# Where in a row the moved activations start: 256 columns at 32 bytes past a multiple of 64, 512 columns at a multiple of 64

## What is computed

```python
def first_block(x, mem, ...):
    mem_n = _rmsnorm(mem, mem_norm_w)
    for l in range(DEPTH):                                    # DEPTH = 1
        h = h + _hybrid_mixer(_rmsnorm(h, mix_norm_w[l]), ...)            # w_in, w_out
        h = h + _memory_cross_attn(_rmsnorm(h, xattn_norm_w[l]), mem_n, ...)   # wq, wk, wv, wo
        h = h + _conv_ffn(_rmsnorm(h, ffn_norm_w[l]), ffn_up[l], ffn_conv_w[l], ffn_down[l])
    return _rmsnorm(h, final_norm_w)

def swiglu(h, w_gu, w_down):
    gate, up = jnp.split(h @ w_gu, 2, axis=-1)
    return (jax.nn.silu(gate) * up) @ w_down

def ffn_half_step(x, mods, g, w_gu, w_down):
    shift, scale, gate = mods
    return x + 0.5 * gate * swiglu(modulated_norm(x, g, shift, scale), w_gu, w_down)

def second_block(x, c, ctx, c_ctx, ...):
    for l in range(DEPTH_2):                                  # DEPTH_2 = 2
        x = ffn_half_step(x, mx[0:3], ...); ctx = ffn_half_step(ctx, mc[0:3], ...)
        # l = 0: Fourier and gating mixer of x and of ctx; l = 1: attention of x over x and ctx
        x = x + mx[5] * out_x
        x = ffn_half_step(x, mx[6:9], ...)
        if not last:
            ctx = ctx + mc[5] * out_c
            ctx = ffn_half_step(ctx, mc[6:9], ...)
    return rms_norm(x, g_final)
```

## Time and profile before

| | before |
|---|---|
| median of three runs (lowest, highest) | 2164.09 us (2163.41, 2167.21) |
| the profiled execution: its own time, its span | 2168.27 us, 2166.5 us |
| TensorE busy in the span | 2098.2 us (97%), 13881 records |
| VectorE, ScalarE, GpSimd busy | 985.2, 817.4, 224.9 us |
| mean granted TensorE clock | 0.991 |
| read from HBM | 310.87 MB, mean 144 GB/s |

### The profile page before, as it was taken

One profiled execution on the slowest core, in us unless ns is written; L12 is line 12 of the kernel. 1 busy time (PEld: TensorE's weight loads), 2 busy tenths in 40 slices (PEclk: granted clock), 3 DMA queues, 4 the chain that ended last, 5 costly groups with the idle time before them and its releaser, 6 DMA issues.

```text
span 2166.5 us, 31783 instructions
## 1 busy us (share of the span) xinstructions
PE 2098.2 (97%) x13881; PEld 1821.0 (84%) x13882; DVE 985.2 (45%) x1270; ACT 817.4 (38%) x1046; POOL 224.9 (10%) x185
## 2 busy tenths in 40 slices
PE   7988999999999999999999999999999999999998
PEld 6985998999978888788887888888788888869998
DVE  6768555767522322354542332253233235645444
ACT  5742454555522222244332222243212224345444
POOL 1000001413101011100101001111100110001011
PEclk9999999999999999999999999999999999999999
DMA  6425544454631333452343332243334222364543
GB/s 236 156 80 195 209 180 180 167 190 158 222 150 67 112 148 114 158 206 98 126 156 132 114 113 82 94 156 136 137 126 155 76 93 93 114 253 156 173 177 109
DMA packets 53708, 313.97 MB, mean 145 GB/s; under 512 B 5952, under 2 KB 12353, under 8 KB 23745
## 3 DMA queue, kind: packets, MB, share of 16 engines
q1 hardware_dynamic: 50848, 308.99, 39.7%
q10 hardware_dynamic: 2720, 2.95, 0.4%
HBM read 310.87 MB, written 1.05 MB: 144 GB/s over the span
## 4 chain that ended last, share of the span: by engine, by line
PE 87%; DVE 6%; ACT 3%; issue 2%; DMA 0%; SPq 0%; POOL 0%; DVEq 0%; ACTq 0%; POOLq 0%
PE psum L258 27%; PE psum L260 26%; PE psum L259 26%; PE psum L1646 3%; ACT w_hi L234 2%; DVE w_lo L242 1%; PE psum L1293 1%; PE psum L1283 1%; PE psum L1307 0%; DMA raw<-in_w_in_r 0%; PE psum L895 0%; DVE xn_lo L1811 0%; PE psum L896 0%; DVE work L431 0%; PE psum L1714 0%
## 5 line engine op out<-in xcount | busy, mean ns | idle before, releaser
L258 PE MATMUL psum<-xn_hi,w_hi 128*128 128x256 f32 (+1 forms) x2600 | 864.5, 332 | 18.2 <-DVE xn_lo L438 8.4
L259 PE MATMUL psum<-xn_lo,w_hi 128*128 128x256 f32 (+1 forms) x2600 | 853.1, 328 | 0.0
L260 PE MATMUL psum<-xn_hi,w_lo 128*128 128x256 f32 (+1 forms) x2600 | 852.7, 328 | 0.0
L242 DVE TENSOR_TENSOR w_lo<-raw,w_hi 128x2048 fp32r<-128x2048 f32 (+1 forms) x246 | 510.0, 2074 | 453.2 <-ACT w_hi L234 452.3
L258 PEld LDWEIGHTS psum<-xn_hi,w_hi 128*128 128x128 f32 x2600 | 496.6, 191 | 74.4 <-issue 23.1
L259 PEld LDWEIGHTS psum<-xn_lo,w_hi 128*128 128x128 f32 x2600 | 497.1, 191 | 43.1 <-issue 1.2
L260 PEld LDWEIGHTS psum<-xn_hi,w_lo 128*128 128x128 f32 x2600 | 496.9, 191 | 42.2
L234 ACT ACTIVATE w_hi<-raw 128x2048 fp32r<-128x2048 f32 (+1 forms) x246 | 421.7, 1714 | 212.8 <-PE psum L260 134.8
L258 PE MATMUL psum<-h_hi,w_hi 128*128 128x512 f32 (+1 forms) x913 | 312.5, 342 | 1.6 <-POOL h_lo L1621 1.6
L259 PE MATMUL psum<-h_lo,w_hi 128*128 128x512 f32 (+1 forms) x913 | 310.9, 341 | 0.0
L260 PE MATMUL psum<-h_hi,w_lo 128*128 128x512 f32 (+1 forms) x913 | 310.8, 340 | 0.0
(11 more groups left out here) (375 smaller groups left out, 1334.6 us busy)
## 6 DMA issues: line engine op xcount, KB each, us to landing
raw<-in_mod SPq DMA_DIRECT2D x72, 1024.0 KB, 4.9
raw<-in_a_up SPq DMA_DIRECT2D x42, 1024.0 KB, 4.9
raw<-in_b_up SPq DMA_DIRECT2D x42, 1024.0 KB, 4.9
raw<-in_ffn_up SPq DMA_DIRECT2D x22, 1024.0 KB, 4.9
raw<-in_a_down SPq DMA_DIRECT2D x32, 704.0 KB, 4.1
raw<-in_b_down SPq DMA_DIRECT2D x32, 704.0 KB, 4.1
raw<-in_ffn_down SPq DMA_DIRECT2D x16, 704.0 KB, 4.1
raw<-in_wo SPq DMA_DIRECT2D x8, 1024.0 KB, 5.0
```

Of the source, the lines that this page charges most:

```text
L242: dve.tensor_tensor(w_lo[:, slot, 0:size], raw[:, raw_slot(("main", g)), 0:size], w_hi[:, slot, 0:size].bitcast(F32), ALU.subtract).then_i ...
L258: pe.matmul(out, lh, rh, start=first, stop=False, skip_group_check=group)
L259: pe.matmul(out, lh, rl, start=False, stop=False, skip_group_check=group)
L260: return pe.matmul(out, ll, rh, start=False, stop=last, skip_group_check=group)
```

## The change

The rows of xn_hi and xn_lo become 528 columns long (2112 bytes, a multiple of 64). Where the normed activations are moved 256 columns at a time they are written and read 8 columns (32 bytes) further on: columns 8 to 263 for X, 264 to 519 for C. Where they are moved 512 at a time they stand 16 columns (64 bytes) further on, 16 to 527. The hidden values of the two narrow feed-forwards stand at columns 8 to 263 of h_hi and h_lo, whose rows stay 512 long; the wide ones stay at 0. q2 and the halves of wide jobs read 256 columns out of a wide row, at a multiple of 64. The memory's values for wv, which are stationary there, lie at the narrow place. To make room, mrow becomes columns 7680 to 7935 of the tensor work.

The rows of the program are the same on every engine, in the same order with the same waits; only in the Fourier and gating branch two writes each of ScalarE and VectorE over two k read 128x2x512 in place of 128x1024.

The diff, cut; what is left out puts one of the new slices in place of X, C, XC or `0:self.w` in the same way:

```diff
+NARROW_AT, WIDE_AT = 8, 16
...
-        xn_hi = sb("xn_hi", [P, KT, 2 * T], F32R)
-        xn_lo = sb("xn_lo", [P, KT, 2 * T], F32R)
+        xn_hi = sb("xn_hi", [P, KT, 2 * T + WIDE_AT], F32R)
+        xn_lo = sb("xn_lo", [P, KT, 2 * T + WIDE_AT], F32R)
...
-        mrow = sb("mrow", [P, 256])
+        mrow = work[:, 7680:7936]
...
+        NARROW_X = slice(NARROW_AT, NARROW_AT + T)
+        NARROW_C = slice(NARROW_AT + T, NARROW_AT + 2 * T)
+        WIDE_X = slice(WIDE_AT, WIDE_AT + T)
+        WIDE_XC = slice(WIDE_AT, WIDE_AT + 2 * T)
...
+                self.at = span.start + (WIDE_AT if wide else NARROW_AT)
...
-                        t, o = slice(h * T, (h + 1) * T), slice(self.span.start + h * T, self.span.start + (h + 1) * T)
+                        t, o = slice(h * T, (h + 1) * T), slice(self.at + h * T, self.at + (h + 1) * T)
...
+                self.xn_span = WIDE_XC if w > T else NARROW_X
+                self.h_span = XC if w > T else NARROW_X
...
-                        pe_feature_major(pe, up, xn_hi, xn_lo, slice(0, self.w))
+                        pe_feature_major(pe, up, xn_hi, xn_lo, self.xn_span)
...
-                    pe_feature_major(pe, down, h_hi, h_lo, slice(0, self.w), n_tiles=1, k_tiles=HALF, before_k=hidden_k,
+                    pe_feature_major(pe, down, h_hi, h_lo, self.h_span, n_tiles=1, k_tiles=HALF, before_k=hidden_k,
...
-                        out = h_hi[r, s.c:s.c + 1, 0:self.w]
+                        out = h_hi[r, s.c:s.c + 1, self.h_span]
...
-                t = slice(h * T, (h + 1) * T)
+                t, o = slice(h * T, (h + 1) * T), slice(WIDE_AT + h * T, WIDE_AT + (h + 1) * T)
...
-                act.activation(xn_hi[:, k, :], o_t[:, k, :], ACT.Copy).then_inc(o_hi, 1)
+                act.activation(xn_hi[:, k, WIDE_XC], o_t[:, k, :], ACT.Copy).then_inc(o_hi, 1)
...
-            pe_feature_major(pe, jobs["w_out"], xn_hi, xn_lo, X, before_k=mixed_k)
+            pe_feature_major(pe, jobs["w_out"], xn_hi, xn_lo, NARROW_X, before_k=mixed_k)
...
-            pe_token_major(pe, jobs["wv"], C)
+            pe_token_major(pe, jobs["wv"], NARROW_C)
...
-            pe_feature_major(pe, jobs["q2"], xn_hi, xn_lo, X, after_chunk=beside_queries)
+            pe_feature_major(pe, jobs["q2"], xn_hi, xn_lo, WIDE_X, after_chunk=beside_queries)
```

More of the change, by code:

```diff
@@ L322, in build, with __init__ @@
             made, scaled, split, squared, added = 0, 0, 0, 0, 0
-            def __init__(self, span, scale, shift=None, out=None, tiles=1, direct=None, pool_low=False, early_table=False, first_tile=None):
+            def __init__(self, span, scale, shift=None, out=None, tiles=1, direct=None, pool_low=False, early_table=False, first_tile=None,
+                         wide=False):
                 self.pool_low = pool_low
@@ L446, in pool_lows @@
                     pool.wait_ge(n_hi, self.split_base + k + 1)
-                    pool.tensor_tensor(xn_lo[:, k, self.span], nrm[:, k, 0:self.w], xn_hi[:, k, self.span].bitcast(F32),
+                    o = slice(self.at, self.at + self.w)
+                    pool.tensor_tensor(xn_lo[:, k, o], nrm[:, k, 0:self.w], xn_hi[:, k, o].bitcast(F32),
                                        ALU.subtract).then_inc(n_lo, 1)
@@ L1210, in post_act_high @@
             act.wait_ge(post_scaled, i + 1)
-            act.activation(xn_hi[:, pair(i), X], z[:, pair(i), :], ACT.Copy).then_inc(post_hi, 1)
+            act.activation(xn_hi[:, pair(i), NARROW_X], z[:, pair(i), :], ACT.Copy).then_inc(post_hi, 1)
         def post_pe_sums(pe, i):
@@ L1700, in __init__ @@
             def __init__(self, scale, shift, job, tiles=1):
-                super().__init__(XC, scale, shift, tiles=tiles)
+                super().__init__(XC, scale, shift, tiles=tiles, wide=True)
                 self.job, self.i = job, HalfNorm.count
@@ L1717, in pe_last @@
             def pe_last(self, pe, s, act_hi, act_lo, n_tiles, k_tiles, k_order):
+                first = WIDE_AT if act_hi is xn_hi else 0
                 for h in range(2):
-                    t = slice(h * T, (h + 1) * T)
+                    t = slice(first + h * T, first + (h + 1) * T)
                     for n in range(n_tiles):
@@ L1926, in pe_first @@
                 for h, t in ((1, C), (0, X)):
+                    o = slice(WIDE_AT + t.start, WIDE_AT + t.stop)
                     for k in k_order:
@@ L2326, in _ @@
             pe.wait_ge(at_lo, att1.heads)
-            pe_feature_major(pe, jobs["wo"], xn_hi, xn_lo, X, in_halves={3: pe_tile_by_tile})
+            pe_feature_major(pe, jobs["wo"], xn_hi, xn_lo, NARROW_X, in_halves={3: pe_tile_by_tile})
             ffn.pe(pe)
@@ L2337, in _ @@
             feed3.pe(pe, late=lambda: mod_turn(pe), closing=n24)
-            pe_feature_major(pe, jobs["k2"], xn_hi, xn_lo, XC, in_halves={0: n24.pe_first})
+            pe_feature_major(pe, jobs["k2"], xn_hi, xn_lo, WIDE_XC, in_halves={0: n24.pe_first})
             def turn_keys():
@@ L2383, in _ @@
             pe.wait_ge(at_lo, att1.heads + att2.heads)
-            pe_feature_major(pe, jobs["wo2"], xn_hi, xn_lo, X, in_halves={3: pe_tile_by_tile})
+            pe_feature_major(pe, jobs["wo2"], xn_hi, xn_lo, NARROW_X, in_halves={3: pe_tile_by_tile})
             n25.pe(pe)
```

55 lines of the change are left out of this document (27 added, 28 removed).

## The result

| | before | after |
|---|---|---|
| median (lowest, highest) | 2165.01 us (2163.41, 2167.61), 6 runs | 2176.09 us (2171.32, 2178.86), 6 runs |
| ratio of the runs | | 1.0045, 95% interval 1.0034 to 1.0055 |
| the profiled execution's time, its span | 2168.27, 2166.5 | 2172.27, 2170.5 |
| mean granted TensorE clock | 0.991 | 0.993 |

A forecast was written before the change was run, and what follows sets the result against it. TensorE's matmul pace was taken as the bound: 4848 x 3.0 ns = 14.5 us off, under 1 us back for first writes, 1 us at risk, giving 2149.6 us from 2164.1; forecast's own range 2132 to 2159, whole range 2110 to 2180.

The forecast's parts named there:

- What bounds the kernel: Whole program: TensorE busy for 97% of the span; the 256-column stages go at the pace of the matmul.
- The extra 13.3 ns: Each full-clock three-pass matmul: 120 ns against 106.7 for 256 columns, 227 against 213.3 for 512; laid to feeding the array.
- 4848 matmuls, from 120 to 117 ns: 256-column matmuls with xn or h moving from the new start: 3.0 ns less each, 14.5 us in all.
- two reads that come to rest against each other: Weight load and moved stream overlap and settle at 120 ns; moving one by 32 bytes (3.3 ns) could give 116.7.
- 227 ns for 512 columns and 120 ns in q2, both as before: Expected profile of the changed kernel: wide matmuls and q2 keep their paces.
- the longer rows: Rows of 528 split writes of two k into two pieces of 512 in the Fourier branch; only six subtractions there.
- the bound of one more piece of 64 bytes: High bound for a moved 256-column matmul: 17 pieces touched instead of 16, so 126.7 ns.
- 14.5 us of gain: Narrow stages: 4848 x 3.0 ns off; first feed-forward's up half from 64.7 to 63.1 us.
- one (109 ns): Rival: the whole feed overhead goes in the 4848 matmuls, pace 109.3 ns, 51.9 us less, 2112; chance 0.14.
- Two (no effect): Rival: the feed reads 256 columns equally fast from any start; 2164 within 5 us; chance 0.19.
- Three: Rival: one more 64-byte piece for each of the 4848 narrow matmuls, 6.67 ns each, 32.3 us slower, 2196; chance 0.19.
- mrow, writes, the stationary side: mrow's copy unchanged; first writes at the new place perhaps 1 us; 192 value-projection matmuls of the first attention priced at nothing.

The follow-up runs named there:

- ahead_32: The kernel before with 32 unused bytes ahead of the raw buffers, so weights and activations all move 32 bytes on together; 2165.1 us, ratio 0.9997.
- rows_528: The changed kernel with both offsets set to 0: xn rows 528 columns long, every moved start a multiple of 64 bytes; 2175.7 us, 1.0040 of before.
- behind_64: The kernel before with 64 unused bytes between the split weights and all tensors behind them, so activations start 64 bytes further on; 2165.0 us, ratio 1.0003.
- behind_32: The kernel before with 32 unused bytes between the split weights and all tensors behind them, so activations start 32 bytes further on; 2185.8 us, ratio 1.0091.
- weights_0: The kernel before with the split weights as one tensor 128 columns longer and mrow in work, weights at their old places; 2165.7 us, ratio 1.0002.
- weights_32: weights_0 with the narrow stages' split weights 32 bytes further on, activations and wide stages' weights unmoved; 2160.7 us, 0.9977 of before.

## Why the prediction was wrong, step by step

- **What bounds the kernel:** right. TensorE's pace decides, and both signs went into the time.
- **The extra 13.3 ns are a matter of feeding:** borne out so far as they change with addresses alone; what in the feed it is was not shown.
- **4848 matmuls, from 120 to 117 ns:** the size was right for the 1056 with h moving (116.7). For the 3792 with xn moving it was 118.2, so 1.8 ns where I had 3.0; together about 10 us by pace in place of 14.5. The reason was only half right. I took the start "32 bytes past a multiple of 64" for the cause; ahead_32 has it and stays at 120, rows_528 and behind_64 have it not and go at 117. My picture of two reads that come to rest against each other fits the distance between weights and activations, and the two beats of behind_64 too, but no run shows the reads.
- **The step that failed:** "227 ns for 512 columns and 120 ns in q2, both as before". The wide matmuls had no term at all; I asked only what a shift of 32 bytes does to the 4848, and priced the longer rows as two split writes. With 2112 bytes from k to k the distance to the weights, which lie 512 bytes apart, changes with k, and the wide matmuls lost 5.0 ns each: 3217 x 5.0 = 16 us. I kept the bound of one more piece of 64 bytes (6.7 ns) for the narrow ones only. The first chunk of q2 shows the same omission the other way: its start stayed at a multiple of 64, and it went at 5.49 / 47 = 117 ns (1847.10 to 1852.59 us), not 120.
- **14.5 us of gain:** mis-sized at the stage level. The paces give 12 us, the stages 8 to 10; some is lost where TensorE waits. The first up half of the first feed-forward, 64.7 us for which I had named 63.1, takes 64.3 in after (362.56 to 426.87 us). There every second chunk of before had 301 to 321 ns from its last start to the next chunk's first, and after has 368 to 387: the wait at the chunk's end takes part of what the matmuls save.
- **Rivals:** one (109 ns) did not come; no distance tried gave less than 116.7 as a mean, and the lowest beat that held was 113.4, in parts of behind_64. Two (no effect) came only as the sum of two effects, in behind_64. The 298 against 291 ns that I read for it are durations; the starts of the token-major matmuls were 119.9 ns apart in before. Three had the sign of the time right for the wrong matmuls: the loss is on the 512-column ones. Its price of 6.67 ns is nearly what they pay in behind_32 (226.8 to 233.3), but behind_64 pays 2.3, so the count of pieces is not shown.
- **mrow, writes, the stationary side:** nothing measurable for mrow, by weights_0. The writes take as long at the new place: 32 of ScalarE at a median of 417 ns before and after, 24 of VectorE at 418 and 420. The token-major matmuls went from 119.9 to 118.2 ns in after, among them the 192 of the first attention's value projection, which I priced at nothing, from 120.0 to 117.8.

## What to carry to other kernels

When a change touches a layout, list every reader of the tensor with its count, those whose own start seems unchanged too, and give each a term: here the 3240 matmuls that were left alone by the stated purpose decided the sign. Read the pace, first start to last start over a stretch without waits, for each width before and after; two opposite changes of 2 to 3% in it are invisible in busy times and can cancel in the total. And test an address hypothesis with a pad ahead of everything and a pad between the two operands: the pair tells an absolute effect from a relative one in two runs.

## What the runs showed of the hardware

- Three-pass matmuls in float32r, weights loaded anew for each: the distance between the start of the moved operand and that of the weights changes the steady pace, and a shift of both together does not. With 256 columns: 119.8 ns at 0, 116.9 at 32 bytes, 117.2 at 64, 119.9 at 96, 118.9 at 128, 118.4 at -32. With 512 columns: 226.8, 233.3, 229.1, 233.3 and 232.5 at 0 to 128, and 233 at -32 in the one chunk of weights_32. So the two widths want opposite things. These are means: at 64 bytes 256 columns go at 113.4 in one stage and at 117.9 in another.
- In before nearly every matmul starts 120 (wide: 226 or 227) ns behind the one ahead of it; at other distances most steps are spread, from 113 to 126 and from 225 to 241. What makes the even beat good for 512 columns and bad for 256 stays open; so do distances between the multiples of 32, and 160 and 192 (-32 is 224).
- The Trainium skill, on its page TensorE: Matmul & The Clock Gate in Part 2, says that stream and weight load have read ports of their own and that loading weights takes no read bandwidth from the running matmul. The runs qualify this in so far as the place of one against the other is worth up to 3 ns in 120 and 6.5 in 227; that does not say at which port.
